# Seven block products for eight in a quarter of the second FFN's input projection, with weight sums added by GpSimd's transfers

## What is computed

```python
def _swiglu(x, w_in, w_out):
    a, b = jnp.split(x @ w_in, 2, axis=-1)
    return (jax.nn.silu(a) * b) @ w_out

u = _modulate(_rmsnorm(h, norm3_g[l]), sh3, sc3)
h = h + 0.5 * gt3 * _swiglu(u, ffn2_w_in[l], ffn2_w_out[l])
```

## Time and profile before

| | us |
|---|---|
| median of 3 runs | 2074.32 |
| span of the profiled execution, first to last instruction | 2071.4 |
| PE busy | 2049.4 (99%) |
| PE weight loads | 1692.2 (82%) |
| VectorE busy | 1655.5 (80%) |
| ScalarE busy | 1060.3 (51%) |
| GpSimd busy | 4.6 (0%) |

### The profile page before, as it was taken

How to read it: one execution, slowest core, us unless ns; L and a number is a source line. 1 busy time by engine, 2 the same in 40 slices (tenths; PEclk the granted TensorE clock), 3 DMA queues, 4 the chain that set the end, 5 groups by cost and what they waited for, 6 DMA issues and landing times.

```text
span 2071.4 us, 24015 instructions
## 1 busy us (share of the span) xinstructions
PE 2049.4 (99%) x9295; PEld 1692.2 (82%) x9295; DVE 1655.5 (80%) x2065; ACT 1060.3 (51%) x1403; POOL 4.6 (0%) x22
## 2 busy tenths in 40 slices
PE   7999999999999999999999999999999999999998
PEld 6888888888888888888777888888888888888887
DVE  6998998888789889888877898979975566755676
ACT  4676434565345565446545675554443444434454
POOL 0000000000000000000000000000000000000000
PEclk9999999999999999999999999999999999999999
DMA  9999999998899769975555687568766555556554
GB/s 369 387 386 321 330 325 330 332 346 283 305 333 339 263 245 343 326 265 178 169 163 164 237 290 275 201 237 303 283 224 201 186 202 185 201 186 201 186 180 162
DMA packets 249601, 540.78 MB, mean 261 GB/s; under 512 B 11920, under 2 KB 14352, under 8 KB 248720
## 3 DMA queue, kind: packets, MB, share of 16 engines
q1 hardware_dynamic: 248400, 539.11, 74.3%
q10 hardware_dynamic: 1088, 0.15, 0.0%
HBM read 537.10 MB, written 2.11 MB: 260 GB/s over the span
## 4 chain that ended last, share of the span: by engine, by line
PE 96%; DMA 2%; DVE 1%; SPq 0%; issue 0%; ACT 0%; DVEq 0%
PE pa L752 14%; PE pb L752 14%; PE pa L760 14%; PE pb L760 14%; PE pb L756 14%; PE pa L756 13%; DMA raw<-in_ffn_w_in_dram 1%; PE pa L1004 1%; PE pb L995 1%; PE pb L1004 1%; PE pb L1000 1%; PE pa L995 1%; PE pa L1000 1%; PE pa L767 1%; DMA ada_s<-in_w_ada_dram 1%; DVE ada_acc L1817 0%
## 5 line engine op out<-in xcount | busy, mean ns | idle before, releaser
L1267 ACT CAST hi<-raw 128x1024 fp32r<-128x1024 f32 x726 | 746.3, 1034 | 875.7 <-PE pb L760 403.4
L1797 DVE TENSOR_TENSOR lo<-raw,hi 128x1024 fp32r<-128x1024 f32 x726 | 859.8, 1197 | 339.8 <-ACT hi L1267 337.3
L1896 DVE SCALAR_TENSOR_TENSOR ada_acc<-ada_w,cond,ada_acc 128x1024 f32<-128x1024 f32 (+1 forms) x240 | 275.3, 1147 | 6.6 <-DVE ada_acc L1896 0.5
L752 PE MATMUL pa<-hi,act_hi 128*128 128x512 f32 x896 | 244.4, 393 | 0.0
L752 PE MATMUL pb<-hi,act_hi 128*128 128x512 f32 x896 | 242.7, 393 | 0.0
L760 PE MATMUL pb<-lo,act_hi 128*128 128x512 f32 x896 | 239.5, 389 | 0.0
L760 PE MATMUL pa<-lo,act_hi 128*128 128x512 f32 x880 | 235.9, 389 | 0.0
L756 PE MATMUL pb<-hi,act_lo 128*128 128x512 f32 x880 | 235.4, 389 | 0.0
L756 PE MATMUL pa<-hi,act_lo 128*128 128x512 f32 x816 | 218.4, 389 | 0.0
L760 PEld LDWEIGHTS pb<-lo,act_hi 128*128 128x128 f32 x896 | 168.2, 188 | 35.0
L752 PEld LDWEIGHTS pb<-hi,act_hi 128*128 128x128 f32 x896 | 166.7, 188 | 35.8 <-issue 2.2
(11 more groups left out here) (390 smaller groups left out, 1955.8 us busy)
## 6 DMA issues: line engine op xcount, KB each, us to landing
raw<-in_ffn_w_in_dram SPq DMA_DIRECT2D x175, 1024.0 KB, 5.2
ada_w<-in_w_ada_dram SPq DMA_DIRECT2D x224, 512.0 KB, 6.2
raw<-in_ffn_w_out_dram SPq DMA_DIRECT2D x64, 1024.0 KB, 5.1
raw<-in_w_in_dram SPq DMA_DIRECT2D x63, 1024.0 KB, 5.2
ada_s<-in_w_ada_dram SPq DMA_DIRECT2D x64, 512.0 KB, 11.7
raw<-in_ffn_w_out_dram SPq DMA_DIRECT2D x32, 768.0 KB, 4.5
raw<-in_w_out_dram SPq DMA_DIRECT2D x16, 1024.0 KB, 5.2
raw<-in_w_att_up_dram SPq DMA_DIRECT2D x8, 1024.0 KB, 5.2
```

The costliest lines, as they stand in the source:

```text
L752: pe.matmul(bank[:, tt, cols], a_hi[:, k0 + kk, tok], w_hi[:, kk, cols], start=start and kk == 0, stop=False, skip_group_check=on)
L1267: act.copy(hi_of(ph, i, j, half)[:, 0:n, 0:w], raw_of(ph, i, j)[:, 2 * half:2 * half + n, 0:w])\
L1797: dve.tensor_tensor(lo_of(ph, i, j)[:, s, 0:w], raw_of(ph, i, j)[:, s, 0:w], hi_of(ph, i, j, half)[:, 0:n, 0:w].bitcast(F32), ALU.subtract)\
L1896: ins = dve.scalar_tensor_tensor(out=acc, in0=wt, scalar=cond[:, kt:kt + 1], in1=acc, op0=ALU.mult, op1=ALU.add)
```

## The change

In each of the 7 groups the first four row blocks (512 of 2048, a quarter of the contraction) for both token tiles and both halves A and B form a product of 2 x 2 by 2 x 2 blocks, a block being 128 tokens x 256 features of u, or 256 features x 512 columns of w. Instead of 8 block products there are 7 (Winograd's form of Strassen's scheme). They need four sums of blocks of u, made once (`s_sums`, `s_casts`, `s_rest` in `ffn2_out0`), and four sums of blocks of weights in every group, T1 to T4:

T3 = w(rows 2-3, B) + w(rows 0-1, B), T1 = w(rows 0-1, B) + w(rows 0-1, A), T2 = w(rows 0-1, A) + T3, T4 = w(rows 2-3, A) + T2.

GpSimd makes the sums by DMAs that add to what lies in SBUF (`fast_sums`). The other three quarters stay in plain units, 12 a group in place of 16, and 6 chunks in place of 8.

```diff
-            plan_phase(f"ffn{f}_in{p}", g, 8, g, 0, g)
+            plan_phase(f"ffn{f}_in{p}", g, 6 if f == 2 and p > 0 else 8, g, 0, g)
...
-    BY_DVE = [plan[name].nat0 + i for name, n in (("ffn2_in0", PARTS[0]), ("ffn2_in1", PARTS[1]),
-                                                  ("ffn2_in2", PARTS[2] - 1)) for i in range(n)]
-    BY_ACT = [plan[name].nat0 + i for name, n in (("ffn1_in1", PARTS[1]), ("ffn1_in2", PARTS[2] - 1), ("up", 3))
+    BY_DVE = [plan["ffn2_in0"].nat0 + i for i in range(PARTS[0])]
+    BY_ACT = [plan[name].nat0 + i for name, n in (("ffn1_in1", PARTS[1]), ("ffn1_in2", PARTS[2] - 1), ("up", 3),
+                                                  ("ffn2_in1", PARTS[1]), ("ffn2_in2", PARTS[2] - 1))
               for i in range(n)]
+    B11, T1, T2, T3, B21, T4, B22 = range(7)
...
+            def load_pair(f, ab):
+
+                if f == 0:
+                    sp.wait_ge(ada_done, len(TILES))
+                else:
+                    sp.wait_ge(x_used, PRODUCTS * (f - 1) + (B22 if ab else T4) + 1)
+                g = PARTS[0] + f
+                if f == 0:
+                    sp.wait_ge(s_lo_ok, 1)
+                for o, k, of in ((T2, 0, 0), (T4, 2, 0), (T3, 2, 1)):
+                    if of == ab:
+                        sp.dma_start(fast_raw(o), w_ffn_in[2][:, k:k + 2, bass.ds(g * NC + ab * FF, NC)]).then_inc(t_in[o], 16)
+                sp.dma_start(pair[:, ab, :, :], w_ffn_in[2][:, 0:4, bass.ds(g * NC + ab * FF, NC)]).then_inc(pair_in[ab], 16)
...
+                            for j in range(6):
+                                if j == 5 and i + 1 < plan[name].n:
+                                    load_pair(FAST[name] + i + 1, 0)
+                                    load_pair(FAST[name] + i + 1, 1)
+                                fast_chunk(plan[name], i, i + g0, j)
+                            return
...
+            def fast_sums(f):
+
+                g = PARTS[0] + f
+                b11 = w_ffn_in[2][:, 0:2, bass.ds(g * NC, NC)]
+                b12 = w_ffn_in[2][:, 0:2, bass.ds(g * NC + FF, NC)]
+                pool.wait_ge(t_in[T3], 16 * (f + 1))
+                pool.dma_start(fast_raw(T3), b12, accum_op=ALU.add).then_inc(t_sum[T3], 16)
+                pool.wait_ge(pair_in[1], 16 * (f + 1))
+                pool.dma_start(fast_raw(T1), b11, accum_op=ALU.add).then_inc(t_sum[T1], 16)
+                pool.wait_ge(t_in[T2], 16 * (f + 1))
+                pool.wait_ge(t_sum[T3], 16 * (f + 1))
+                pool.dma_start(fast_raw(T2), fast_raw(T3), accum_op=ALU.add).then_inc(t_sum[T2], 16)
+                pool.wait_ge(t_in[T4], 16 * (f + 1))
+                pool.wait_ge(t_sum[T2], 16 * (f + 1))
+                pool.dma_start(fast_raw(T4), fast_raw(T2), accum_op=ALU.add).then_inc(t_sum[T4], 16)
...
+                product(f, B11, pa[:, 1, :], *a11, start=True)
+                pe.wait_ge(s_lo_ok, 1)
+                product(f, T1, pm[:, :], *s1, start=True)
+                pe.wait_ge(v_moved, COPIES * f + 1)
+                product(f, T2, pa[:, 1, :], *s2)
+                run(0, (0,))
+                pe.wait_ge(v_moved, COPIES * f + 3)
+                product(f, T3, pa[:, 1, :], *s3)
+                run(1, (0,))
+                pe.wait_ge(v_moved, COPIES * f + 4)
+                run(0, (1,))
+                run(1, (1,))
+                product(f, B21, pa[:, 0, :], *a12)
+                product(f, T4, pa[:, 1, :], *a22)
+                run(2)
+                pe.wait_ge(pb_seed, f + 1)
+                product(f, B22, pb[:, 0, :], *s5)
+                for n_ in range(3, 12):
+                    run(n_)
...
+                for n_, j, half, k0 in fast_units():
+                    split(ph, i, j, half, 2)
+                    if n_ == 3:
+                        fast_copy(f, B11, pa[:, 0, :], pa[:, 1, :])
+                        fast_cast(f, B21)
+                        fast_copy(f, T1, q5[:, :], pm[:, :])
+                        fast_copy(f, T2, px[:, 0, :], pa[:, 1, :])
+                        fast_cast(f, T4)
+                        fast_cast(f, B22)
+                        fast_copy(f, T3, px[:, 1, :], pa[:, 1, :])
...
+                    if i + 1 < ph.n and n_ >= 8:
+                        fast_cast(f + 1, n_ - 8)
...
+            def fast_rest(f, o):
+
+                dve.wait_ge(x_hi, PRODUCTS * f + o + 1)
+                if o in (T2, T3):
+                    dve.wait_ge(t_sum[T4 if o == T2 else T2], 16 * (f + 1))
+                dve.tensor_tensor(fast_lo(o), fast_raw(o), fast_hi(o).bitcast(F32), ALU.subtract).then_inc(x_lo, 1)
```

More of the change, by code:

```diff
@@ L463, in slot_of @@
         def slot_of(ph, i, j):
[L465 removed]
+            return 0 if at_seam(ph, i, j - 1) else (ph.c0 + ph.per * i + j) % RING
         def raw_of(ph, i, j):
@@ L487, in hi_of, with fast_raw, fast_lo, fast_hi @@
             return hi[:, (2 * j + half) % 4, :, :]
+        def fast_raw(o):
+            return {B11: pair[:, 0, 0:2, :], B21: pair[:, 0, 2:4, :], T1: pair[:, 1, 0:2, :], B22: pair[:, 1, 2:4, :],
+                    T2: t23[:, 0, :, :], T3: t23[:, 1, :, :], T4: t4[:, :, :]}[o]
+        def fast_lo(o):
+            return {B11: pair_lo[:, 0, 0:2, :], B21: pair_lo[:, 0, 2:4, :], T1: pair_lo[:, 1, 0:2, :],
+                    B22: pair_lo[:, 1, 2:4, :], T2: t23_lo[:, 0, :, :], T3: t23_lo[:, 1, :, :], T4: t4_lo[:, :, :]}[o]
+        def fast_hi(o):
+            return hi_a[:, :, :] if o % 4 == 3 else hi_b[:, o % 4, :, :]
+        def fast_units():
+            for n_ in range(12):
+                j, half = divmod(n_, 2)
+                yield n_, j, half, 4 + 4 * (j % 3) + 2 * half
         def over(eng, n, body):
@@ new lines, in fast_body @@
+            def fast_body(name, i, mid):
+                ph, f = plan[name], FAST[name] + i
+                for n_, j, half, k0 in fast_units():
+                    split(ph, i, j, half, 2)
+                    if n_ == 3:
+                        if i > 0:
+                            hidden(ph, i - 1)
+                            turn_square(ph.nat0 + i - 1)
+                        else:
+                            mid(3)
+                        fast_rest(f, B21)
+                        fast_rest(f, T4)
+                        fast_rest(f, B22)
+                        fast_seed(f)
+                    if i > 0 and n_ == 7:
+                        nat_evac(ph.nat0 + i - 1, i - 1)
+                    if i + 1 < ph.n and n_ >= 7:
+                        if n_ >= 8:
+                            fast_rest(f + 1, n_ - 8)
@@ L2287, in out_phase @@
                                 add_out(ph, b - 1, gate)
+                        if name == "ffn2_out0" and (b, n_) == (1, 5):
+                            s_sums()
+                        if name == "ffn2_out0" and (b, n_) == (1, 7):
+                            s_rest()
+                        if name in ("ffn2_out0", "ffn2_out1"):
+                            f = FAST["ffn2_in1" if name == "ffn2_out0" else "ffn2_in2"]
+                            if b == 3 and n_ in (1, 4, 5, 6):
+                                fast_rest(f, {1: B11, 4: T1, 5: T2, 6: T3}[n_])
                         if name == "ffn2_out2" and b > 0 and n_ == 6:
```

131 lines of the change are left out of this document (127 added, 4 removed).

## The result

| | before | after |
|---|---|---|
| median of the runs, us | 2074.32 | 2121.44 (2118.16 to 2122.58) |
| span of the profiled execution | 2071.4 | 2118.3 |
| granted TensorE clock, mean | 0.999 | 0.991 |

What follows compares the result with a forecast made beforehand. PE's matmuls were taken as the bound (busy 99%). Span 2071.4 - 9.5 (matmuls) + 1.5 (hand-overs) = 2063.4, plus 2.9 from span to median: 2066.3 us; range from 2064.8 less half a us of scatter to 2104.

Steps and rivals of the forecast that it cites:

- The matmuls: On PE in the 7 fast groups: 186 matmuls a group for 192, 42 fewer, a gain of 9.5 us.
- the copies at a group's start: ScalarE's copies for B11, T2, T3: each has 0.5 us to spare, taken as nothing; missing by 0.3 each costs 6.3 us.
- `fin_row`: Its load moves to `ffn2_out2`, wanted only after several units there: nothing.
- SyncE's queue: Five new DMAs between chunks 4 and 5; chunk 5 lands at 28.4, wanted at 28.6: nothing on the path.
- the slow rival: At VectorE's wait for T4's sum before unit 11's rest: additions of 7.0 us, 2090 us; chance of slower 0.41.
- a = 5.2 us for an addition: Time of one GpSimd addition from its wait to its landing, taken from a 1024 KB load.
- the prediction's own formula: Stall a group at unit 11's `lo`: 22.9 (T3's load) + 3a - 38.8 (T4's sum due); -0.3 forecast.
- The rival's 7.0: Addition time from 1024 KB at a DMA share of 0.96: stall 5.1 us in 5 groups, 2090 us.
- its limit of 7.95: Addition time if each also waits out a whole chunk (5.2 + 2.75): stall 8.0 us a group, 2105 us.
- The share of 0.58: DMA share before the change, cited against the slow rival: queues empty between chunks.
- ScalarE's queue the laxer one: T2's cast, with unit 11's behind it, needs T2's sum by 37.3, which allows additions of 7.2 us.
- upper case: A whole chunk's wait before every addition, 2105 us; the range ends just short of it, at 2104.

Runs made afterwards that it cites:

- experiment 1: The changed kernel without GpSimd's additions: T1 to T4 stay plain loaded blocks, the sums of weights left out; 2065.08 us, ratio 0.9958.
- experiments 9 and 10: The kernel before with ten (9) or eight (10) more VectorE instructions ahead of the last unit's subtraction in five groups; 2111.25 and 2094.04 us.
- experiment 4: The kernel before with five GpSimd transfers of 512 KB (copies and additions), six times, into buffers nothing waits for; 2073.93 us.
- experiment 2: The changed kernel with GpSimd's four additions turned into plain copies, same order and waits; 2103.22 us, ratio 1.0142.
- experiment 5: The changed kernel with T3's and T2's blocks loaded early, ahead of chunk 4, and T2 added before T1; 2087.64 us, ratio 1.0066.
- experiment 6: experiment 5 with the casts and rests of T1, T2, T3 moved behind unit 11; 2068.23 us, ratio 0.9973.
- experiment 7: experiment 5 with T1's block loaded early too and added right behind T3, casts where the change has them; 2080.85 us, ratio 1.0036.
- experiment 8: experiment 7 with the loads ahead of parts two and three spread over three successive chunk slots; 2070.03 us, ratio 0.9981.

## Why the prediction was wrong

**Right.** The matmuls: 42 fewer, 9.5 us forecast, 8.7 by experiment 1 beside its own runs of before (2073.8 - 2065.1). VectorE, ScalarE's total, the copies at a group's start (no hole there in any of the seven groups), `fin_row` and SyncE's queue in the change itself (the first block 0.8 us later than worked out, chunks in time): nothing, as forecast. The place and mechanism of the slow rival: VectorE's wait for T4's sum ahead of unit 11's rest, a hole on `lo` in 5 of 7 groups.

**Wrong, the step that failed: a = 5.2 us for an addition.** It was the landing of a 1024 KB load by SyncE. In the chain the three took 10.35, 8.46 and 5.79 us with their hand-overs (1631.50 to 1641.85, to 1650.31, to 1656.10), 24.6 in all against 15.6. In the prediction's own formula, 23.7 + 24.6 - 38.8 gives a stall of 9.5 us a group for its -0.3; times five, 2074.3 - 9.5 + 47.5 = 2112. The slow matmuls that follow VectorE's hole, some 2 us each by experiments 9 and 10, bring it to about 2122, where 2121.4 was measured.

Two things are in the 9 us between 15.6 and 24.6. Some 3.5 us are there beside chunk loads alone (experiment 4, an estimate of 19 us): with that chain the same formula gives a stall of about 4 us a group, more than the whole gain. The other 5 us or so are the company. The rival's 7.0, from loads in a full queue, was nearer, and even its limit of 7.95, a whole chunk's wait, lies below the mean of 8.2. The share of 0.58 that spoke against it is an average of the kernel before; while T3's and T2's additions run it is 1.08 and 1.06. Of the 56 us, adding itself holds 18 (14 to 23, experiment 2).

The Trainium skill's rule that a reducing transfer runs at half the rate (Collectives: The Full Stack, "The bandwidth ceiling") points the right way, but its factor is not what these rows show: beside chunk loads alone the addition landed in 5.7 us within SBUF where the copy took 3.9, and giving up the adding took away 18 of 56 us. Its fit for GpSimd's DMAs (DMA: Bandwidth & Descriptors, "Anatomy of one DMA"), an estimate of 3.2 us for 512 KB, disagrees with the 5.5 to 6.7 us of the copies from HBM in experiment 4, and is nearer to the 3.9 within SBUF.

**Missing: ScalarE at T1.** The prediction called ScalarE's queue the laxer one, and looked there only at T2's cast. T1's cast stands ahead of unit 10's, wanted at 36.7 less two casts of 1 us, so by about 34.6; T1's sum came at 37.4. In the change itself this added nothing that the chain shows: the DMAs of T3, T2 and T4 run on while PE stands, T4's sum comes at 48.2 after the earlier hole is long over, and the chain that ended last passes by ScalarE. It counts once T4's sum is early: it alone left 15.4 us of holes in experiment 5, and moving the cast (experiment 6) or loading T1 early (experiment 7) took them away.

**Missing: the slow matmuls behind a hole.** No term had them. They are 17.8 us in all, shown as a cost of holes by experiments 9 and 10; those behind ScalarE's holes hide in the wait for T4's sum too, and an estimated 2 us a group behind VectorE's count. The earlier trace rows could not show it, as PE had no hole in that stretch. The range ended at 2104 since its upper case had a of 7.95 and not 8.2, T3's load at 22.9 and not 23.7, and nothing for the clock.

**Still open.** How the 5 us that the chain loses to its company divide between the pairs, the blocks and the chunks. T1's addition is hardly the reason, since T3's and T2's took as long in experiment 6, where T1's is issued behind both. No experiment puts the same transfers on another queue, so what GpSimd's queue itself adds is open too. A second set of buffers for pairs and sums, with which the additions would have a whole group of 42 us, was not tried, nor is it shown that it would fit.

## What to carry to other kernels

Cost a serial chain of transfers by a row of the same queue and the same neighbours, hand-over included; where none exists, let the range hold well more than a plain load of the bytes moved (here 5.2 us was taken and 8.2 measured), and ask of every instruction that waits for the chain what stands behind it in its queue. A wait that nobody needs before the next stage belongs behind the last work of this one: moving two loads 7 to 11 us up, T2's addition ahead of T1's, and three casts with their rests back turned +47 us into -6 us, with the same transfers. Where two queues stall in the same group, the later wait sets the time: ask what is left when it is gone before you count the earlier one. To an operand's lateness add what the clock takes: a hole of 2.5 us cost 4.3, one of 5.0 cost 7.6.

## What was not expected of the hardware

- Issuing an adding transfer keeps GpSimd 1.21 us from HBM and 0.86 to 0.90 within SBUF, where a plain copy takes 0.74 and 0.58 (the change and experiment 4).
- GpSimd's plain 512 KB from HBM landed in 5.4 us (median of each series' second copy in experiment 4), while SyncE's 1024 KB in the same stretch took 5.1. With the change's loads beside it, its adding transfers of 512 KB have median landings of 7.9 to 10.7 us.
- The DMA share does not tell what is moved: 1.10 at 260 GB/s from 1570 to 1575 us in experiment 7, where additions run, against 1.05 at 388 GB/s from 155 to 160 us in the changed kernel, where none does.
- A single hole of 2.5 us on PE, after hundreds of us without one, is followed by some eight matmuls near the 1.2 GHz level (experiment 10). Behind holes of 1.3 and 1.1 us in experiment 8 the granted clock stays at 1.00.
